# Gate and up weights in 4 MB transfers from the ninth expert on, and a shorter shift of the shared down piece

## The chip, the cores and the metric

The kernel runs on one NeuronCore of one Trainium2 chip. The metric is the device time of that core in microseconds (us). Everything is float32.

## What is computed

A transformer block on 256 tokens of width 1024: a token mixer (sparse attention beside an mLSTM), a cross-attention to 256 memory tokens, and a mixture of 32 experts with the top 4 chosen per token. The change concerns the experts alone. For every expert `e`, in the reference:

```
def expert_block(args):
    xb, e = args
    gu = xb @ w_gu[e] + b_gu[e]
    g, u = gu[:, :D_FF], gu[:, D_FF:]
    g = jnp.minimum(g, SWIGLU_LIMIT)
    u = jnp.clip(u, -SWIGLU_LIMIT, SWIGLU_LIMIT)
    return ((u + 1.0) * (g * jax.nn.sigmoid(SWIGLU_ALPHA * g))) @ w_down[e] + b_down[e]
```

`w_gu[e]` is 1024 x 2048 (8 MB) and `w_down[e]` is 1024 x 1024 (4 MB), so the 32 experts read 32 x 12 MB of weights, each byte once.

## The kernel before, in words

The mixer and the cross-attention come first. Then come 32 expert blocks, numbered here from 0, one for each expert, with 64 token slots each; the text says "block 14" for the work on expert 14. In a block TensorE multiplies the gathered tokens (`r_memT`, the stationary operand, 128 x 64) with the weights as moving operand: four gate-and-up pieces `gu0` to `gu3` (16 matmuls of 128 x 512 each, two rows `k` of the contraction per partition), then the scatter of the block before (L1377), two turns of the places (L1484), the gather of tokens for a later block (L1361, not in blocks 30 and 31), the transposes of the hidden values (L1489), the biases (L1458), then two down pieces `dn0` and `dn1`. Between the last gate-and-up piece and `dn0` VectorE and ScalarE compute the activation; TensorE's own work fills most of that time.

Each piece is one transfer of 2 MB: 128 partitions with one unbroken run of 16 KB each. SyncE (SP) issues all of them on one queue, served in order, and each transfer is spread over 16 DMA engines, 8 runs on each.

The buffers for weights are 11 slots of 2 MB. Even experts use `gu0` to `gu3` and `dn0` in `ring` (semaphores `loaded[s]`, `freed[s]`), odd experts use `r_odd[0]` to `r_odd[3]` for `gu0` to `gu3` and a part of `r_gbx` for `dn0` (`odd_loaded[j]`, `odd_freed[j]`). The eleventh slot, in `ring`, holds `dn1` of every expert: the shared down piece. The first five pieces of an expert are called its heads here. Before SP issues a piece it waits until TensorE has used what stood in that slot (two experts earlier for heads, one expert earlier for `dn1`); all that stands behind it in SP's program waits with it.

The order of the queue is written out by hand. In its first part (up to expert 11's heads) `dn1` of expert e stands behind all five heads of expert e + 1, so that TensorE gets `dn1` late. Then a shift: in each of five steps `dn1` moves one piece forward. After it `dn1` of an expert stands right behind its own heads.

```
for k in range(1, HEADS + 1):
    e = 2 * AHEAD + 1 + k
    if k > 1:
        heads(e, range(HEADS + 1 - k, HEADS))
    if k < HEADS:
        heads(e + 1, range(HEADS - k))
    others(e)
```

`others(i)` waits for the shared slot and issues `dn1` of expert i. `piece_rows` is where TensorE waits for a piece. For expert 31 `gu3`, `dn0` and `dn1` come in halves.

Of the kernel before, what the change touches and what calls it, by code (L numbers as in the profile page):

```python
# [40 lines left out]
NE, TOPK = 32, 4  # L41
SLOTS = 64
# [32 lines left out]
AHEAD = 5  # L75

# [78 lines left out]
def program(nc, A, out):  # L155
    ctx = ExitStack()
    with ctx:
# [11 lines left out]
        r_odd = [sb(f"r_odd{j}", [P, SLOT_W]) for j in range(4)]  # L169
# [150 lines left out]
        x_rows = r_x[:].rearrange("p (t j q k) -> p t j k q", t=TT, j=4, k=2)  # L320
# [99 lines left out]
        gu_dram = A["w_gu"].rearrange("l e (j p k) n -> (l e) j p k n", k=2, p=P)  # L420
# [7 lines left out]
        def _(sp):  # L428
# [67 lines left out]

            def expert_piece(e, j):
                name = EXPERT_PIECES[j]
                s = eslot[name]
                if j < 4:  # L500
                    dst, src = ring[:, s].rearrange("p (k n) -> p k n", k=2), gu_dram[e, j]
                else:
                    dst, src = ring[:, s].rearrange("p (k n) -> p k n", k=4), dn_dram[e, j - 4]
# [7 lines left out]
            def odd_half(e, j, k):  # L511
                sp.dma_start(odd_slot[j][:, k], gu_dram[e, j][:, k]).then_inc(odd_loaded[j], 16)

            def odd_piece(e, j):
                sp.dma_start(odd_slot[j], gu_dram[e, j] if j < 4 else dn_dram[e, j - 4]).then_inc(odd_loaded[j], 16)  # L515
# [153 lines left out]
        def _(act):  # L669
# [136 lines left out]
            act.dma_start(gain2.rearrange("p (j k) -> p j k", k=2), A["g_ffn"][0].rearrange("(j p k) -> p j k", p=P, k=2))\  # L806
# [1376 lines left out]
```

## Time and profile before

| | |
|---|---|
| time, median of 3 runs | 1281.8 us (1279.98 to 1282.27) |
| profiled execution, its own time | 1279.55 us |
| its span | 1277.8 us |
| mean granted TensorE clock | 0.995 of full speed |
| TensorE busy (matmuls) | 1227.0 us, 96% |
| VectorE, ScalarE, GpSimd busy | 25%, 11%, 1% |
| DMA over the span | 454.69 MB, mean 356 GB/s |

The span is measured from the first to the last instruction of one profiled execution. The busy share of matmuls includes the pipelining of one matmul into the next, so 96% doesn't mean that nothing can be gained elsewhere. The page cuts the span into 40 slices of 32 us; of these the last 28, from about 380 us on, are the expert blocks.

### The profile page before, as it was taken

Reading aid. Unit: us, or ns where it says so; the run is one execution under the profiler, and the core shown is the slowest. Engines: PE = TensorE matmul, PEld = TensorE weight load, DVE = VectorE, ACT = ScalarE, POOL = GpSimd, SP = SyncE. Lnnn points to the kernel's source line nnn. Section 1 sums busy time; section 2 is a strip of 40 time slices with the busy share of each in tenths; the row PEclk is TensorE's granted clock in tenths of the full one; section 3 lists DMA queues with packets and bytes.
Section 4 is the critical chain, followed back from the end, with each engine's and each line's share of the span. In section 5 each row is a group of like instructions: output and inputs, shape, how many; then the busy total and the mean of one; then the engine's idle time right before and its main releaser. Section 6 shows DMA issues by size and latency. Waiting matters only on the chain.

```text
span 1277.8 us, 14901 instructions
## 1 busy us (share of the span) xinstructions
PE 1227.0 (96%) x6163; PEld 603.2 (47%) x6163; DVE 324.3 (25%) x733; ACT 145.2 (11%) x325; POOL 8.1 (1%) x34
## 2 busy tenths in 40 slices
PE   9999999999999999999989999999998999999987
PEld 8868885858544333334333333433333344333322
DVE  2362334370732111212111111211111132211112
ACT  2223332002210000000000000000000000000001
POOL 1000000000000000000000000000000000000000
PEclk9999999999999999999999999999999999999999
DMA  9953233257489999999999999999999999999996
GB/s 333 310 214 132 83 116 132 99 202 278 169 341 429 425 430 428 426 428 427 430 429 428 428 427 431 429 428 427 427 430 430 428 426 427 428 428 427 427 428 270
DMA packets 60595, 454.69 MB, mean 356 GB/s; under 512 B 7244, under 2 KB 14088, under 8 KB 35080
## 3 DMA queue, kind: packets, MB, share of 16 engines
q1 hardware_dynamic: 58312, 452.49, 86.2%
q10 hardware_dynamic: 2240, 1.58, 0.4%
q8 instruction: 33, 0.54, 0.2%
q14 instruction: 10, 0.08, 0.0%
HBM read 453.00 MB, written 1.05 MB: 355 GB/s over the span
## 4 chain that ended last, share of the span: by engine, by line
PE 70%; DMA 28%; SPq 1%; DVE 1%; issue 1%; ACT 0%; DVEq 0%; ACTq 0%
PE ps L1384 32%; DMA r_odd<-in_w_gu_dram 16%; PE ps L914 13%; DMA ring<-in_w_down_dram 12%; PE ps L1234 4%; PE ps L921 3%; PE ps L1361 3%; PE ps L1377 3%; PE ps L1458 2%; PE ps L967 1%; PE ps L1489 1%; PE ps L1484 1%; PE ps L1305 1%; PE ps L1287 1%; SPq L515 1%
## 5 line engine op out<-in xcount | busy, mean ns | idle before, releaser
L1384 PE MATMUL ps<-ring,r_memT 128*64 128x512 f32 x1024 | 225.8, 594 | 13.2 <-DMA ring<-in_w_gu_dram 12.4
L1384 PE MATMUL ps<-r_odd,r_memT 128*64 128x512 f32 x1024 | 225.4, 594 | 12.5 <-DMA r_odd<-in_w_gu_dram 12.5
L1384 PE MATMUL ps<-ring,r_kx 128*64 128x512 f32 x768 | 176.9, 609 | 13.0 <-DMA ring<-in_w_down_dram 13.0
L2080 DVE TENSOR_SCALAR r_ga<-ps 128x512 f32<-128x512 f32 x32 | 22.1, 692 | 636.7 <-PE ps L1384 636.7
L1384 PEld LDWEIGHTS ps<-r_odd,r_memT 128*64 128x64 f32 x1024 | 72.9, 137 | 162.5 <-issue 135.6
L1384 PEld LDWEIGHTS ps<-ring,r_memT 128*64 128x64 f32 x1024 | 71.9, 137 | 161.3 <-issue 135.6
L914 PE MATMUL ps<-r_odd,ring 128*128 128x256 f32 x576 | 128.0, 380 | 0.0
L1384 PEld LDWEIGHTS ps<-ring,r_kx 128*64 128x64 f32 x768 | 54.9, 140 | 132.3 <-issue 108.3
L914 PEld LDWEIGHTS ps<-r_odd,ring 128*128 128x128 f32 x576 | 108.5, 190 | 16.8 <-issue 2.3
L855 ACT ACTIVATE r_ga<-r_ga 128x512 f32<-128x512 f32 x32 | 20.2, 630 | 460.0 <-DVE r_ga L2080 460.0
L1361 PE MATMUL ps<-r_dm,r_x 128*128 128x128 f32 x512 | 65.8, 282 | 0.0
L1377 PE MATMUL ps<-r_kx,r_dm 64*128 64x512 f32 x256 | 63.6, 615 | 0.7 <-ACT r_kx L861 0.7
L1361 PEld LDWEIGHTS ps<-r_dm,r_x 128*128 128x128 f32 x512 | 62.8, 197 | 1.6 <-DVE r_dm L2010 0.8
L1384 PE MATMUL ps<-r_gbx,r_kx 128*64 128x512 f32 x256 | 58.5, 598 | 0.8 <-DVE r_kx L2093 0.8
L861 ACT ACTIVATE r_kx<-ps 128x512 f32<-128x512 f32 x32 | 19.1, 597 | 335.9 <-PE ps L1384 335.9
L1377 PEld LDWEIGHTS ps<-r_kx,r_dm 64*128 64x128 f32 x256 | 22.0, 186 | 41.3 <-issue 39.7
L2018 DVE TENSOR_TENSOR r_memT<-ps,sm 128x512 f32<-128x512 f32 x32 | 22.1, 692 | 64.6 <-PE ps L1361 64.6
L1384 PEld LDWEIGHTS ps<-r_gbx,r_kx 128*64 128x64 f32 x256 | 17.0, 136 | 40.6 <-issue 27.4
L1458 PE MATMUL ps<-r_ga,r_kx 32*64 32x512 f32 x256 | 35.8, 612 | 0.0
L914 PE MATMUL ps<-r_memT,ring 128*128 128x256 f32 x128 | 28.5, 381 | 0.0
L1234 PE MATMUL ps<-ring,r_odd 128*128 128x512 f32 x64 | 27.8, 592 | 0.0
L914 PEld LDWEIGHTS ps<-r_memT,ring 128*128 128x128 f32 x128 | 24.0, 190 | 3.8 <-issue 0.7
(358 smaller groups left out, 834.1 us busy)
## 6 DMA issues: line engine op xcount, KB each, us to landing
ring<-in_w_gu_dram SPq DMA_DIRECT2D x63, 2048.0 KB, 27.0
r_odd<-in_w_gu_dram SPq DMA_DIRECT2D x60, 2048.0 KB, 28.2
ring<-in_w_down_dram SPq DMA_DIRECT2D x47, 2048.0 KB, 22.6
r_gbx<-in_w_down_dram SPq DMA_DIRECT2D x15, 2048.0 KB, 28.5
ring<-in_w_in_dram SPq DMA_DIRECT2D x7, 2048.0 KB, 14.0
r_odd<-in_w_gu_dram SPq DMA_DIRECT2D x8, 1024.0 KB, 14.5
ring<-in_w_k_x_dram SPq DMA_DIRECT2D x2, 2048.0 KB, 10.5
ring<-in_w_v_x_dram SPq DMA_DIRECT2D x2, 2048.0 KB, 8.0
```

The source lines that it names most:

```text
L515: sp.dma_start(odd_slot[j], gu_dram[e, j] if j < 4 else dn_dram[e, j - 4]).then_inc(odd_loaded[j], 16)
L855: nc.scalar.activation(sig, gact, ACT.Sigmoid, scale=1.702).then_inc(sig_done, 1)
L861: nc.scalar.activation(y_slot, ps[:, ZBK, :], ACT.Copy).then_inc(yslot_ready, 1)
L914: last = mm(o[:, j * T:(j + 1) * T], w(k), src[:, k, :], start=(k == 0), stop=(k == kk - 1))
L921: last = mm(o, src[:, k, t * P:(t + 1) * P], w[:, k, 0:n], start=(k == 0), stop=(k == C - 1))
L1234: last = mm(o, lhs(k), rhs[:, k], start=(k == 0), stop=(k == 3), skip_group_check=True)
L1361: last = mm(ps[:, buf, c * P:(c + 1) * P], x_rows[:, t, 2 * q + c // 2, c % 2], place[:, t], start=(t == 0), stop=(t == 1))
L1377: last = mm(ps[:, YB + 2 * t + n, :], scat[half, t * P:(t + 1) * P], y_slot[half, :], start=False, stop=False, skip_group_check=True)
L1384: last = mm(ps[n * SLOTS:(n + 1) * SLOTS, bk, :], stationary_, moving(n), start=start, stop=stop, skip_group_check=True)
L1458: mm(ps[n * SLOTS:(n + 1) * SLOTS, GBK + b, :], cur[q * NE:(q + 1) * NE, :], bgu_rows[q * NE:(q + 1) * NE, :], start=True, stop=False, ski ...
L2018: V.tensor_tensor(xg[:, buf, 4 * q:4 * q + 4], ps[:, bank_, :].rearrange("p (c s) -> p c s", c=4), gain_half[q], ALU.mult).then_inc(xg_rea ...
L2080: V.tensor_scalar(gact, ps[:, GBK, :], 7.0, None, ALU.min).then_inc(g_limited, 1)
```

## The change

Three things change in the transfers, and one in the layout that goes with them.

1. The contraction index of `w_gu` is laid on partitions with four rows per partition instead of two (`(q p k)` with k=4), so that two neighbouring pieces of an expert are one region of 4 MB with 32 KB per partition. For experts 0 to 7 and in part for expert 31 `gu_part` still loads a 2 MB half of it (16 KB out of each 32 KB). From expert 8 on `even_pair` and `odd_pair` load `gu0` with `gu1` and `gu2` with `gu3` in one transfer. To have neighbouring slots the four `r_odd` tensors become one, `r_odds`.
2. SP issues a pair when the second of its two slots is free. TensorE waits for the pair at its first piece, and no longer at the second (`second`).
3. The shift of `dn1` has three steps in place of five: `dn1` of expert 12 stands behind four pieces of expert 13 as before, that of expert 13 behind two pieces of expert 14 (before: three), that of expert 14 directly behind its own heads (before: behind two pieces of expert 15).
4. The gather's stationary operand `x_rows` and the gain `gain2` follow the new index: their elements are taken from `r_x` in steps of 4 (before: 2). TensorE's blocks 4 to 7 stand outside the loop.

```diff
-        gu_dram = A["w_gu"].rearrange("l e (j p k) n -> (l e) j p k n", k=2, p=P)
+        gu_dram = A["w_gu"].rearrange("l e (q p k) n -> (l e) q p k n", k=4, p=P)
...
-        x_rows = r_x[:].rearrange("p (t j q k) -> p t j k q", t=TT, j=4, k=2)
+        x_rows = r_x[:].rearrange("p (t q r k) -> p t q k r", t=TT, q=2, k=4)
...
+            def gu_part(e, j):
+                return gu_dram[e, j // 2][:, 2 * (j % 2):2 * (j % 2) + 2]
+
+            def even_pair(e, q):
+                s = eslot[EXPERT_PIECES[2 * q]]
+                assert eslot[EXPERT_PIECES[2 * q + 1]] == s + 1
+                dst = ring[:, s:s + 2].rearrange("p s (k n) -> p (s k) n", k=2)
+                sp.dma_start(dst, gu_dram[e, q]).then_inc(loaded[s], 16)
+
+            def odd_pair(e, q):
+                dst = r_odds[:, 2 * q:2 * q + 2].rearrange("p s (k n) -> p (s k) n", k=2)
+                sp.dma_start(dst, gu_dram[e, q]).then_inc(odd_loaded[2 * q], 16)
...
-            with sp.Fori(1, AHEAD + 1) as p:
+            def odd_pairs(p):
+                for q in range(2):
+                    sp.wait_ge(odd_freed[2 * q + 1], p)
+                    odd_pair(p * 2 + 1, q)
+                sp.wait_ge(odd_freed[4], p)
+                odd_piece(p * 2 + 1, 4)
...
-            for k in range(1, HEADS + 1):
+            def part_of(e, k):
+                if k == 2:
+                    s = eslot["dn0"]
+                    sp.wait_ge(odd_freed[4] if e % 2 else freed[s], e // 2)
+                    odd_piece(e, 4) if e % 2 else expert_piece(e, 4)
+                else:
+                    sp.wait_ge(odd_freed[2 * k + 1] if e % 2 else freed[eslot[EXPERT_PIECES[2 * k + 1]]], e // 2)
+                    odd_pair(e, k) if e % 2 else even_pair(e, k)
+
+            for k in range(1, 4):
                 e = 2 * AHEAD + 1 + k
-                if k > 1:
-                    heads(e, range(HEADS + 1 - k, HEADS))
-                if k < HEADS:
-                    heads(e + 1, range(HEADS - k))
+                for part in range(4 - k, 3):
+                    if k > 1:
+                        part_of(e, part)
+                for part in range(3 - k):
+                    part_of(e + 1, part)
                 others(e)
...
-            for j in range(HEADS):
-                sp.wait_ge(odd_freed[j], NE // 2 - 1)
-                if j < 3:
-                    odd_piece(NE - 1, j)
-            in_halves(odd_slot[3], gu_dram[NE - 1, 3], 2, odd_loaded[3], rest_loaded[0])
+            sp.wait_ge(odd_freed[1], NE // 2 - 1)
+            odd_pair(NE - 1, 0)
+            sp.wait_ge(odd_freed[3], NE // 2 - 1)
+            odd_piece(NE - 1, 2)
+            in_halves(odd_slot[3], gu_part(NE - 1, 3), 2, odd_loaded[3], rest_loaded[0])
+            sp.wait_ge(odd_freed[4], NE // 2 - 1)
...
-            def piece_rows(j, uses, odd):
-
+            def piece_rows(j, uses, odd, paired=True, last_expert=False):
+
+                second = paired and j in (1, 3)
                 if odd and j < HEADS:
-                    pe.wait_ge(odd_loaded[j], uses * 16 + (32 if j < 3 else 16))
+                    if j == 3 and last_expert:
+                        pe.wait_ge(odd_loaded[3], ALONE // 2 * 16 + 16)
+                    elif not second:
+                        pe.wait_ge(odd_loaded[j], uses * 16 + (32 if j < 3 else 16))
                     return lambda k, a: odd_slot[j][:, k, a:a + 512]
                 s = eslot[EXPERT_PIECES[j]]
-                pe.wait_ge(loaded[s], uses * 16 + (16 * dmas[s] + 16))
+                if not second:
+                    pe.wait_ge(loaded[s], uses * 16 + (16 * dmas[s] + 16))
...
-            four_blocks(0)
-            with pe.Fori(1, 6) as n:
+            for n in range(ALONE // 4):
+                four_blocks(n)
+            with pe.Fori(ALONE // 4, 6) as n:
                 four_blocks(n)
```

On SP, the shift in the kernel before begins with four pieces of expert 13; then come `dn1` of 12, `dn0` of 13, three pieces of expert 14, `dn1` of 13, `gu3` and `dn0` of 14, two pieces of 15 and `dn1` of 14 (`ring<-in_w_down_dram` is `dn1` of any expert and `dn0` of an even one, `r_gbx<-in_w_down_dram` is `dn0` of an odd one):

```order
L515 DMA r_odd<-in_w_gu_dram 128x4096 x4
L504 DMA ring<-in_w_down_dram 128x4096
L515 DMA r_gbx<-in_w_down_dram 128x4096
L504 DMA ring<-in_w_gu_dram 128x4096 x3
L504 DMA ring<-in_w_down_dram 128x4096
L504 DMA ring<-in_w_gu_dram 128x4096
L504 DMA ring<-in_w_down_dram 128x4096
L515 DMA r_odd<-in_w_gu_dram 128x4096 x2
L504 DMA ring<-in_w_down_dram 128x4096
```

In the changed kernel the same place on SP is the whole shift: both pairs of 13, `dn1` of 12, `dn0` of 13, the first pair of 14, `dn1` of 13, the second pair of 14, and then `dn0` and `dn1` of 14:

```order
L510 DMA r_odds<-in_w_gu_dram 128x8192 x2
L519 DMA ring<-in_w_down_dram 128x4096
L530 DMA r_gbx<-in_w_down_dram 128x4096
L506 DMA ring<-in_w_gu_dram 128x8192
L519 DMA ring<-in_w_down_dram 128x4096
L506 DMA ring<-in_w_gu_dram 128x8192
L519 DMA ring<-in_w_down_dram 128x4096 x2
```

`dn1` of 14 has moved ahead of the two pieces of 15, and `dn1` of 13 ahead of `gu2` of 14.

On TensorE (PE), in the loop over blocks of the kernel before, the gate-and-up part of an even block waits for each of its four pieces (`loaded4`, `loaded5`, `loaded0`, `loaded1` are the slots of `gu0` to `gu3`):

```order
L1384 MATMUL ps<-ring,r_memT 64x512 [waits loaded4]
L1384 MATMUL ps<-ring,r_memT 64x512 x7
L1450 REGISTER_ALU
L1384 MATMUL ps<-ring,r_memT 64x512 [waits loaded5]
L1384 MATMUL ps<-ring,r_memT 64x512 x7
L1450 REGISTER_ALU
L1384 MATMUL ps<-ring,r_memT 64x512 [waits loaded0]
L1384 MATMUL ps<-ring,r_memT 64x512 x7
L1384 MATMUL ps<-ring,r_memT 64x512 [waits loaded1]
```

In the changed kernel the same part of the loop on TensorE has two waits:

```order
L1434 MATMUL ps<-ring,r_memT 64x512 [waits loaded4]
L1434 MATMUL ps<-ring,r_memT 64x512 x15
L1505 REGISTER_ALU
L1434 MATMUL ps<-ring,r_memT 64x512 [waits loaded0]
L1434 MATMUL ps<-ring,r_memT 64x512 x15
```

The waits for `gu1` and `gu3` are gone, and `gu0` now waits until `gu1` is there as well.

## Rows read from the trace of the kernel before

**Rows 1.** The page: GB/s in 40 slices, and TensorE's down matmuls

```profile
GB/s 333 310 214 132 83 116 132 99 202 278 169 341 429 425 430 428 426 428 427 430 429 428 428 427 431 429 428 427 427 430 430 428 426 427 428 428 427 427 428 270
L1384 PE MATMUL ps<-ring,r_kx 128*64 128x512 f32 x768 | 176.9, 609 | 13.0 <-DMA ring<-in_w_down_dram 13.0
```

**Rows 2.** DMA packets of two expert blocks, 960 to 1018.74 us

```profile
DMA packets 1728, 25.17 MB, mean 428 GB/s; under 512 B 192, under 2 KB 192, under 8 KB 192
```

**Rows 3.** DMA packets from 50 to 60 us, rows of 2 KB

```profile
DMA packets 1918, 3.87 MB, mean 387 GB/s; under 512 B 30, under 2 KB 30, under 8 KB 1918
```

**Rows 4.** The chain of waits, transfer of `dn1` of block 11: start, length

```profile
675.03 25.49 DMA ring<-in_w_down_dram
```

**Rows 5.** SP in time: issues of dn1 of 12, 13, 14

```profile
705.95 0.33 SPq L504 DMA_DIRECT2D ring<-in_w_down_dram  x1
...
732.39 0.33 SPq L504 DMA_DIRECT2D ring<-in_w_down_dram  x1
...
758.81 0.33 SPq L504 DMA_DIRECT2D ring<-in_w_down_dram  x1
```

**Rows 6.** TensorE at `dn1` of blocks 7, 8, 10, 11: start, length, [idle before]

```profile
583.07 3.65 PE L1384 MATMUL ps<-ring,r_kx 128*64 128x512 f32 x16 [1.01 <-DMA ring<-in_w_down_dram]
...
612.45 5.31 PE L1384 MATMUL ps<-ring,r_kx 128*64 128x512 f32 x16 [2.72 <-DMA ring<-in_w_down_dram]
...
671.20 3.65 PE L1384 MATMUL ps<-ring,r_kx 128*64 128x512 f32 x16 [2.71 <-DMA ring<-in_w_down_dram]
...
700.56 5.35 PE L1384 MATMUL ps<-ring,r_kx 128*64 128x512 f32 x16 [2.73 <-DMA ring<-in_w_down_dram]
```

**Rows 7.** TensorE in a late block, from gu3 on

```profile
960.03 3.65 PE L1384 MATMUL ps<-r_odd,r_memT 128*64 128x512 f32 x16 [1.25 <-DMA r_odd<-in_w_gu_dram]
963.61 1.99 PE L1377 MATMUL ps<-r_kx,r_dm 64*128 64x512 f32 x8
...
969.27 3.65 PE L1384 MATMUL ps<-r_gbx,r_kx 128*64 128x512 f32 x16
...
976.19 7.08 PE L1384 MATMUL ps<-ring,r_memT 128*64 128x512 f32 x32
984.50 3.65 PE L1384 MATMUL ps<-ring,r_memT 128*64 128x512 f32 x16 [1.24 <-DMA ring<-in_w_gu_dram]
...
1018.77 3.65 PE L1384 MATMUL ps<-r_odd,r_memT 128*64 128x512 f32 x16 [1.24 <-DMA r_odd<-in_w_gu_dram]
```

**Rows 8.** SP: two issues into a queue that had run empty

```profile
377.74 0.33 SPq L504 DMA_DIRECT2D ring<-in_w_gu_dram  x1
...
381.17 0.33 SPq L504 DMA_DIRECT2D ring<-in_w_gu_dram  x1
```

**Rows 9.** The same two transfers, 377 to 383 us: time to landing

```profile
ring<-in_w_gu_dram SPq DMA_DIRECT2D x1, 2048.0 KB, 7.7
...
ring<-in_w_gu_dram SPq DMA_DIRECT2D x1, 2048.0 KB, 9.1
```

**Rows 10.** TensorE from gu3 of block 30 to the scatter of block 31

```profile
1225.86 3.65 PE L1384 MATMUL ps<-ring,r_memT 128*64 128x512 f32 x16 [1.24 <-DMA ring<-in_w_gu_dram]
1229.44 1.99 PE L1377 MATMUL ps<-r_kx,r_dm 64*128 64x512 f32 x8
...
1233.52 7.09 PE L1384 MATMUL ps<-ring,r_kx 128*64 128x512 f32 x32
1240.63 3.65 PE L1384 MATMUL ps<-r_odd,r_memT 128*64 128x512 f32 x16
...
1255.84 1.94 PE L1384 MATMUL ps<-r_odd,r_memT 128*64 128x512 f32 x8 [0.15 <-DMA r_odd<-in_w_gu_dram]
1257.71 1.99 PE L1377 MATMUL ps<-r_kx,r_dm 64*128 64x512 f32 x8
```

**Rows 11.** Weight loads in steps of 2 (L1361) and of 4 (L1489)

```profile
L1361 PEld LDWEIGHTS ps<-r_dm,r_x 128*128 128x128 f32 x512 | 62.8, 197 | 1.6 <-DVE r_dm L2010 0.8 <-issue 0.8
...
L1489 PEld LDWEIGHTS ps<-ident,r_kx 128*128 128x128 f32 x128 | 17.8, 204 | 0.7 <-DVE r_kx L2089 0.7
```

More of the change, by code:

```diff
@@ L75 @@
 AHEAD = 5
+ALONE = 8
 FILL = [("ga", n) for n in range(4)] + [("gb", n) for n in range(4)] + \
@@ L168, in program @@
         r_x = sb("r_x", [P, TT * D])
-        r_odd = [sb(f"r_odd{j}", [P, SLOT_W]) for j in range(4)]
+        r_odds = sb("r_odds", [P, 4, SLOT_W])
+        r_odd = [r_odds[:, j] for j in range(4)]
         r_gbx = sb("r_gbx", [P, 1672 + SLOT_W])
@@ L500, in expert_piece @@
                 if j < 4:
-                    dst, src = ring[:, s].rearrange("p (k n) -> p k n", k=2), gu_dram[e, j]
+                    dst, src = ring[:, s].rearrange("p (k n) -> p k n", k=2), gu_part(e, j)
                 else:
@@ L511, in odd_half @@
             def odd_half(e, j, k):
[L512 removed]
+                sp.dma_start(odd_slot[j][:, k], gu_part(e, j)[:, k]).then_inc(odd_loaded[j], 16)
             def odd_piece(e, j):
[L515 removed]
+                sp.dma_start(odd_slot[j], gu_part(e, j) if j < 4 else dn_dram[e, j - 4]).then_inc(odd_loaded[j], 16)
             def odd_heads(p, part=range(HEADS)):
@@ L560, in _, with even_pairs @@
             sp.wait_ge(first_half_freed, 1)
-            sp.dma_start(rows2[:, 0], gu_dram[2, 0][:, 0]).then_inc(first_half_loaded, 16)
+            sp.dma_start(rows2[:, 0], gu_part(2, 0)[:, 0]).then_inc(first_half_loaded, 16)
             sp.wait_ge(freed[s], 1)
-            sp.dma_start(rows2[:, 1], gu_dram[2, 0][:, 1]).then_inc(loaded[s], 16)
+            sp.dma_start(rows2[:, 1], gu_part(2, 0)[:, 1]).then_inc(loaded[s], 16)
             even_heads(1, range(1, HEADS))
             others(1)
-            with sp.Fori(1, AHEAD + 1) as p:
+            def odd_pairs(p):
[4 more added lines that the diff above has]
+                odd_piece(p * 2 + 1, 4)
+            def even_pairs(p):
+                for q in range(2):
+                    sp.wait_ge(freed[eslot[EXPERT_PIECES[2 * q + 1]]], p)
+                    even_pair(p * 2, q)
+                sp.wait_ge(freed[eslot["dn0"]], p)
+                expert_piece(p * 2, 4)
+            with sp.Fori(1, ALONE // 2 - 1) as p:
                 odd_heads(p)
@@ L605, in _ @@
                     e = sp.value_load(cnt_i[0:1, bass.ds(i - (NE - 1), 1)], min_val=0, max_val=NE - 1)
-                    for j in range(6):
+                    for q in range(2):
+                        sp.wait_ge(freed[eslot[EXPERT_PIECES[2 * q + 1]]], i - NE // 2)
+                        even_pair(e, q)
+                    for j in (4, 5):
                         sp.wait_ge(freed[eslot[EXPERT_PIECES[j]]], i - NE // 2 if j < HEADS else i)
@@ L1360, in gather_half @@
                     for t in range(TT):
-                        last = mm(ps[:, buf, c * P:(c + 1) * P], x_rows[:, t, 2 * q + c // 2, c % 2],
+                        last = mm(ps[:, buf, c * P:(c + 1) * P], x_rows[:, t, q, c],
                                   place[:, t], start=(t == 0), stop=(t == 1))
@@ L1368, in gather_late @@
                     for t in range(TT):
-                        last = mm(ps[:, XBK, c * SLOTS:(c + 1) * SLOTS], x_rows[:, t, c // 2, c % 2],
+                        last = mm(ps[:, XBK, c * SLOTS:(c + 1) * SLOTS], x_rows[:, t, c // 4, c % 4],
                                   place[:, t, 0:SLOTS], start=(t == 0), stop=(t == 1))
@@ L1467, in gate_up @@
                         pe.wait_ge(first_half_loaded, 16)
-                    w = piece_rows(j, heads_used if j < HEADS else i, odd)
+                    w = piece_rows(j, heads_used if j < HEADS else i, odd, not (isinstance(i, int) and i < ALONE),
+                                   is_block(i, NE - 1))
                     for k in range(2):
```

17 lines of the change are left out of this document (13 added, 4 removed).

## The prediction

> **What bounds the kernel now.** I read the page's GB/s line first: from slice 13 to slice 39 every slice moves 425 to 431 GB/s [rows 1]. The queue of weight transfers never pauses in the expert blocks, so their length is bytes over rate plus what stands after the last transfer. Then TensorE in time: in a late block it waits 1.24 us at `gu2` and again at `gu3`, each time for a transfer, and two blocks take 1018.77 - 960.03 = 58.74 us, 29.37 each [rows 7]. TensorE's own work in a block is `gu3` 3.58 (960.03 to 963.61), the middle part 5.66 (to 969.27), the down pieces 6.92 (to 976.19) and three more pieces at 3.46: 26.54 us. It has 2.83 us to spare per block. So only three things can move the time: the rate of the stream, a hole in it, and TensorE's work after the last landings. Last I read how the stream's time divides over packets [rows 2, 3], how SP's issues stand to landings in the shift [rows 4, 5], and the tail [rows 10].
>
> **Term 1, longer runs.** In two late blocks 1728 packets pass, 192 of them the small ones that report completion [rows 2]: 1536 runs of 16 KB, 96 per DMA engine, 58740 / 96 = 611.9 ns each. From 50 to 60 us the queue is full as well, with runs of 2 KB: (1918 - 30) / 16 = 118 runs per engine in 10 us, 84.7 ns each [rows 3]. The difference, 527.2 ns for 14336 bytes, is 27.2 bytes per ns; 2048 bytes then take 75.3 ns and 9.4 ns are left as a gap per run. By this a 2 MB piece takes 8 x 612.0 = 4.90 us and a pair in 32 KB runs 8 x (1205.2 + 9.4) = 9.72 us instead of 9.79. An expert saves 16 gaps, 0.150 us; experts 8 to 30 and one pair of 31 are 23.5 experts: 3.5 us saved. If the completion packets cost a gap too, two fewer per expert and engine add 0.4: 3.9. The lower bound is nothing, if the loss is not per run. I take 3.5, since the two stretches differ in run length above all.
>
> The Trainium skill, page "DMA: Bandwidth & Descriptors", section "Why small descriptors are slow (HBM only)", gives a fixed overhead of about 3 cycles per packet, with 850 MHz in its section "Where 436 GB/s comes from"; as an estimate from that page a gap would be 3.5 ns, the saving 23.5 x 16 x 3.5 = 1.3 us, and my sum below would be 2.2 us higher. The measured gap is nearly three times that, and I go by it.
>
> **Term 2, a hole at the second step of the shift.** SP may issue `dn1` of 14 only when TensorE has used `dn1` of 13. That does not move with the change: TensorE runs without a wait from the landing of `dn1` of 11 (675.03 + 25.49 = 700.52 [rows 4]) to this issue at 758.81 [rows 5], 58.3 us. What the queue still holds does. Before, two pieces of 15 stood ahead of `dn1` of 14; the queue then had twelve pieces after `dn1` of 11 up to `dn0` of 14, and these two: 14 x 4.90 = 68.5 us, 10.2 more than the 58.3. Now the queue ends with `dn0` of 14: four pairs and four single pieces, 4 x 9.72 + 4 x 4.90 = 58.45 us, 0.15 us after the issue. Is that too late? A transfer issued at 377.74 into an empty queue landed after 7.7 us; the next, issued at 381.17 and 4.3 us before that landing, after 9.1, that is 4.8 us behind it [rows 8, 9]. So 4.3 us ahead is early enough, and with nothing ahead 7.7 - 4.9 = 2.8 us of start and report are seen. Taking the hole as 2.8 minus the margin: 2.65 us. But the 58.3 us hold a slow `dn1` of 11: 5.35 us with the granted clock at half in it, where the same work takes 3.65 elsewhere [rows 6]. Of the three waits of 2.7 us shown there two were followed by such a stretch, the third was not; after 1.0 us there was none. Without it TensorE is 1.7 us earlier, the margin is 1.85 and the hole 0.95. Bounds: 0 (engines still at work on the last runs when the new ones come) and 2.8. I take 0.95. The other issues of the shift have room: `dn1` of 13 at 732.39 is 31.9 after the landing of 11 and the queue reaches to 38.9 (three pairs, two pieces); `dn1` of 15 comes 26.4 after that of 14 and the queue grows meanwhile by 29.2. SP's issues for later pairs stand behind it, and none is needed before.
>
> **Term 3, the tail.** Before, TensorE took `gu0` as it landed and had `gu3` alone to do after the last gate-up landing. With pairs it starts both halves when the second is there. Count from the landing of the second pair of 30 (the time at which `gu3` of 30 lands now): two pieces 7.04, then scatter, turns, transposes and biases 4.08 (1229.44 to 1233.52), down pieces 7.11 (to 1240.63) [rows 10]: 18.2 us. The first pair of 31 lands 2 x 4.90 + 9.72 = 19.5 after, so TensorE waits for it. Then four pieces follow without a wait, since `gu2` and the halves of `gu3` are there before they are wanted: 13.9 us, end at 33.45. Before, the scatter of block 31 begins at 1257.71, 31.85 after 1225.86. So 1.6 us lost. If TensorE's clock drops after its wait ahead of that block's second pair, 1.7 more makes 19.9 in place of 19.5, and the loss is 2.0.
>
> In the steady blocks the wait becomes one piece of 29.22 - 26.54 = 2.7 us ahead of the second pair, as long as the waits after which the clock fell in rows 6, and no longer two or more of 1.24. A slow stretch costs 1.7 and fits into the 2.7: the stream still sets the pace. Pairs gated by their second slot are no danger to the stream: `dn1` is used 6.92 + 5.66 + 7.04 us after the second pair landed, 9.8 after its own landing, with 24.4 us of heads queued: 14.5 us ahead.
>
> **Costed at nothing.** `x_rows` in steps of 4: TensorE's weight loads go from 197 to about 204 ns, as those of L1489, which takes such steps [rows 11]; they lie under the matmuls. The first eight blocks are issued as before. TensorE's unrolled code is fetched beside 12 MB per block. The waits dropped at `gu1` and `gu3` would have been fulfilled. If the weight loads had no cover, 7 ns x 512 would be 3.6 us of TensorE time, spread over blocks with 2.7 us to spare.
>
> **Sum.** -3.5 + 0.95 + 1.6 = -1.0 us; with the clock low at both places -3.5 + 2.65 + 2.0 = +1.1. Against the profiled execution's 1279.55 that is 1278.6 to 1280.7; the median of the runs stands 2.25 higher, so 1280.8 to 1282.9. I forecast 1281.0: no change. A measurement of this kernel tells about 0.2%, 2.6 us, from no change.
>
> **Rivals.**
> - *Full saving, nothing given back.* The hole closes, since DMA engines run several packets at once, and the tail's lag shrinks. 3.5 to 3.9 us less: 1277.9 to 1278.3, faster. For it: queue and TensorE miss each other by 0.15 us only. Against: the tail's 1.6 is TensorE's own arithmetic. 0.15.
> - *No saving per run.* A 32 KB run is moved as two packets of 16 KB, or the loss is not per run. Then +0.95 + 1.6 = 2.5, up to 4.6 with the low clock: 1284.3 to 1286.4, slower or at its edge. For it: no run of 32 KB stands in the trace. Against: the 2 KB stretch. Each ns of gap is worth 23.5 x 16 ns = 0.38 us, so with both slow stretches (4.6 without a saving) it decides from a gap below 5 ns. 0.14.
> - *The wider pitch costs rate.* Partitions now read 32 KB apart, engines at once twice as far apart as before. From the rows: each 1% of rate on the pairs is 23.5 x 19.4 x 0.01 = 4.6 us, so a rate lower by 0.8% undoes the saving and turns -1.0 into +2.6, which decides; at 2% it is +8 and the time 1290. For it: nothing in the trace; 2 KB rows at other pitches lose only what the gap explains. 0.07. The Trainium skill, same page, section "Latency and other measured facts", reports copies slowing when partitions lie at large powers of two apart, by about 3% at 512 KiB, and no run here shows that.
> - *The stream starves later.* SP waits for both slots, TensorE lags after its slow stretches and after the extra tables in block 24, and holes of some 3 us come more than once: 1285 to 1288. Against: 14.5 us of queue. 0.06.
> - The forecast: 0.58, of which 0.05 lies beyond -2.6 us and 0.04 beyond +2.6.
>
> **Range and chances.** The range reaches to most of the first two rivals and to the low edges of the others: 1277.6 to 1285.4. Faster 0.15 + 0.05 and a little for a gap above my estimate: 0.22. Slower: 0.04, most of the no-saving case (0.10), 0.07 and 0.06 minus their mild ends: 0.24. Same 0.54.
>
> **What would show it.** Right: packets of 32 KB in the late blocks and a rate near 430; two late blocks in 58.4 us; one wait of 2.7 us per block at the second pair, sometimes followed by a low clock; one slice of the DMA line short near 757 us; SP's issue of `dn1` of 14 with the queue nearly empty; `gu0` to `gu3` of block 31 in one row of some 13.9 us. Wrong: packets still at 16 KB, a rate of 428 or below, more than one hole, or a last block in which TensorE waits for halves of `gu3`.

## The result, and the profile of the changed kernel

The changed kernel takes 1294.27 us (median of 5 runs, 1293.2 to 1295.39) and the kernel before 1281.73 (5 runs, 1279.98 to 1282.27). The ratio is 1.01, its 95% interval 1.0088 to 1.0111: slower by some 12.5 us, which is clear of the noise. The prediction said no change, 1277.6 to 1285.4 us. The times of the kernel before lie in two clusters, near 1279.8 and near 1282.2 us, so that its median jumps between them from one set of runs to the next; below, small differences are therefore read from the ratios, each 0.001 of which is 1.28 us.

From the page of the changed kernel: the span, the busy time of each engine, GB/s in 40 slices of 32.3 us, and the shares of the chain of work that ended last:

```profile
span 1291.4 us, 14741 instructions
PE 1274.6 (99%) x6163; PEld 667.0 (52%) x6163; DVE 324.3 (25%) x733; ACT 145.2 (11%) x325; POOL 8.0 (1%) x34
GB/s 331 317 200 130 98 98 130 98 240 275 163 307 407 426 428 429 428 429 429 434 430 427 424 318 429 435 426 435 427 433 425 430 430 433 428 433 429 430 425 238
PE 94%; DMA 5%; DVE 1%; issue 0%; ACT 0%; SPq 0%; DVEq 0%; ACTq 0%
```

TensorE was busy for 1227.0 us before and is now busy for 1274.6, with the same 6163 matmuls. From the 14th slice on the rate is not lower than before [rows 1], but for one short slice, the 24th (742 to 775 us). The last line is the surprise: the chain runs on TensorE for 94% of the span and hardly touches a DMA (before: 70% and 28%). So the question is which matmuls take 47.6 us more. The groups by line and shape, 365 to 1290 us (busy us, mean ns of one | idle us before them):

```profile
L1434 PE MATMUL ps<-ring,r_memT 128*64 128x512 f32 x1024 | 223.8, 593 | 0.8 <-issue 0.7
L1434 PE MATMUL ps<-r_odds,r_memT 128*64 128x512 f32 x1024 | 222.8, 592 | 2.1 <-DMA r_odds<-in_w_gu_dram 2.1
L1434 PE MATMUL ps<-ring,r_kx 128*64 128x512 f32 x768 | 171.1, 594 | 0.0
L1411 PE MATMUL ps<-r_dm,r_x 128*128 128x128 f32 x512 | 124.8, 397 | 0.0
L1411 PEld LDWEIGHTS ps<-r_dm,r_x 128*128 128x128 f32 x512 | 121.9, 328 | 1.6 <-DVE r_dm L2067 0.8 <-issue 0.8
L1545 PEld LDWEIGHTS ps<-ident,r_kx 128*128 128x128 f32 x128 | 21.3, 228 | 0.5 <-DVE r_kx L2146 0.5
L1540 PEld LDWEIGHTS ps<-ident,r_dm 128*128 128x128 f32 x64 | 6.4, 140 | 24.4 <-issue 24.4
```

The same gather group and TensorE's waits of the kernel before, for comparison (total us, times, longest):

```profile
L1361 PE MATMUL ps<-r_dm,r_x 128*128 128x128 f32 x512 | 65.8, 282 | 0.0
...
PE ps L1384 <- DMA ring<-in_w_down_dram: 13.0, 6, 2.7
PE ps L1384 <- DMA r_odd<-in_w_gu_dram: 12.5, 11, 1.3
PE ps L1384 <- DMA ring<-in_w_gu_dram: 12.4, 10, 1.2
```

The gather, whose stationary operand is now taken from `r_x` in steps of 4, went from 65.8 to 124.8 us: 59.0 us more for 512 matmuls. Its weight loads went from 197 [rows 11] to 328 ns. (The records of neighbouring matmuls overlap, so 282 and 397 ns are not the pace.) Against that TensorE lost 37.9 us in waits for transfers before and 2.1 now. Busy time +47.6 and waits -35.8 give +11.8 us; the last scatter starts at 1281.46 in place of 1269.42, 12.0 later. (Busy time rose by less than 59 mainly because the matmuls on the experts' weights, lines L1384 and L1434, take 676.2 us in sum in place of 686.6: with the waits went the slow-clock stretches behind some of them and the fresh starts behind the others. The granted clock rose from 0.995 to 0.999.)

In time, TensorE in two late blocks of the changed kernel, and the gather of before:

```profile
954.31 3.89 PE L1411 MATMUL ps<-r_dm,r_x 128*128 128x128 f32 x16
...
966.57 13.91 PE L1434 MATMUL ps<-r_odds,r_memT 128*64 128x512 f32 x64
980.41 1.99 PE L1427 MATMUL ps<-r_kx,r_dm 64*128 64x512 f32 x8
982.33 0.44 PE L1540 MATMUL ps<-ident,r_dm 128*128 128x128 f32 x2
982.60 3.89 PE L1411 MATMUL ps<-r_dm,r_x 128*128 128x128 f32 x16
986.33 0.63 PE L1545 MATMUL ps<-ident,r_kx 128*128 128x128 f32 x4
986.89 1.09 PE L1513 MATMUL ps<-r_ga,r_kx 32*64 32x512 f32 x8
...
994.87 13.98 PE L1434 MATMUL ps<-ring,r_memT 128*64 128x512 f32 x64
```

```profile
965.80 2.05 PE L1361 MATMUL ps<-r_dm,r_x 128*128 128x128 f32 x16
967.69 0.63 PE L1489 MATMUL ps<-ident,r_kx 128*128 128x128 f32 x4
```

From gather to gather 982.60 - 954.31 = 28.29 us pass, without a wait. The gather itself lasts 3.73 us to the next operation (982.60 to 986.33), where it was 1.89 (965.80 to 967.69): from the start of one matmul to the next 233 ns in place of 118. Here the answer to a puzzle stands too: 1.84 us more per block is less than the 2.83 us that TensorE had to spare in late blocks [rows 7]. But it did not have them everywhere. In the kernel before the first blocks run at TensorE's own pace of 26.4 us (the scatters of blocks 0 to 4 start at 409.34, 435.75, 462.15, 488.56 and 515.01), living on the pieces loaded ahead, and so do blocks 13 to 17 (the scatters of blocks 12 and 17 start at 746.02 and 878.15, 26.4 per block). Over all 32 blocks the slack was the waits and the slower matmuls behind them, about 37.9 + 10.4 = 48 us, and the edit asked for 59.

### The profile page after: what moved, and what is told of

Read it like the earlier page. It is cut to its first block, busy times and chain, and to the rows that moved or that the text cites. A ratio compares the mean times of both kernels' runs of the same rounds, so it can differ in the third digit from the quotient of the medians.

```text
span 1291.4 us, 14741 instructions
## 1 busy us (share of the span) xinstructions
PE 1274.6 (99%) x6163; PEld 667.0 (52%) x6163; DVE 324.3 (25%) x733; ACT 145.2 (11%) x325; POOL 8.0 (1%) x34
## 4 chain that ended last, share of the span: by engine, by line
PE 94%; DMA 5%; DVE 1%; issue 0%; ACT 0%; SPq 0%; DVEq 0%; ACTq 0%
PE ps L1434 48%; PE ps L964 13%; PE ps L1411 9%; DMA r_odds<-in_w_gu_dram 5%; PE ps L1427 4%; PE ps L1284 4%; PE ps L971 3%; PE ps L1513 2%; PE ps L1545 1%; PE ps L1017 1%; PE ps L1540 1%; PE ps L1355 1%; PE ps L1337 1%; PE ps L1184 0%; PE ps L1249 0%; DMA r_x<-in_x_dram 0%
## 5 line engine op out<-in xcount | busy, mean ns | idle before, releaser
L1434 PE MATMUL ps<-r_odds,r_memT 128*64 128x512 f32 x1024 | 222.8, 592 | 2.1 <-DMA r_odds<-in_w_gu_dram 2.1
L1434 PE MATMUL ps<-ring,r_memT 128*64 128x512 f32 x1024 | 223.8, 593 | 0.8 <-issue 0.7
L1434 PE MATMUL ps<-ring,r_kx 128*64 128x512 f32 x768 | 171.1, 594 | 0.0
L1434 PEld LDWEIGHTS ps<-r_odds,r_memT 128*64 128x64 f32 x1024 | 75.5, 137 | 146.8 <-issue 145.2
L1434 PEld LDWEIGHTS ps<-ring,r_memT 128*64 128x64 f32 x1024 | 74.1, 137 | 144.6 <-issue 142.0
L964 PE MATMUL ps<-r_odds,ring 128*128 128x256 f32 x576 | 128.0, 380 | 0.0
L1411 PE MATMUL ps<-r_dm,r_x 128*128 128x128 f32 x512 | 124.8, 397 | 0.0
L1411 PEld LDWEIGHTS ps<-r_dm,r_x 128*128 128x128 f32 x512 | 121.9, 328 | 1.6 <-DVE r_dm L2067 0.8
L964 PEld LDWEIGHTS ps<-r_odds,ring 128*128 128x128 f32 x576 | 108.5, 190 | 16.8 <-issue 2.3
L1434 PEld LDWEIGHTS ps<-ring,r_kx 128*64 128x64 f32 x768 | 54.7, 137 | 112.9 <-issue 106.4
L1434 PE MATMUL ps<-r_gbx,r_kx 128*64 128x512 f32 x256 | 58.5, 598 | 0.8 <-DVE r_kx L2150 0.8
L1434 PEld LDWEIGHTS ps<-r_gbx,r_kx 128*64 128x64 f32 x256 | 17.2, 136 | 40.6 <-issue 34.0
L1513 PE MATMUL ps<-r_ga,r_kx 32*64 32x512 f32 x256 | 35.8, 612 | 0.0
L964 PE MATMUL ps<-r_memT,ring 128*128 128x256 f32 x128 | 28.5, 381 | 0.0
L1284 PE MATMUL ps<-ring,r_odds 128*128 128x512 f32 x64 | 27.8, 592 | 0.0
## 6 DMA issues: line engine op xcount, KB each, us to landing
r_odds<-in_w_gu_dram SPq DMA_DIRECT2D x8, 1024.0 KB, 14.2
```

Source lines behind the costliest of these rows:

```text
L964: last = mm(o[:, j * T:(j + 1) * T], w(k), src[:, k, :], start=(k == 0), stop=(k == kk - 1))
L1284: last = mm(o, lhs(k), rhs[:, k], start=(k == 0), stop=(k == 3), skip_group_check=True)
L1411: last = mm(ps[:, buf, c * P:(c + 1) * P], x_rows[:, t, q, c], place[:, t], start=(t == 0), stop=(t == 1))
L1434: last = mm(ps[n * SLOTS:(n + 1) * SLOTS, bk, :], stationary_, moving(n), start=start, stop=stop, skip_group_check=True)
L1513: mm(ps[n * SLOTS:(n + 1) * SLOTS, GBK + b, :], cur[q * NE:(q + 1) * NE, :], bgu_rows[q * NE:(q + 1) * NE, :], start=True, stop=False, ski ...
```

## Experiments

**1. Which part costs: the transfers or the gather.** Two kernels. Both take other columns of `r_x` than the weights' rows want, so they compute something else than the reference, and their times alone are read. The first is the changed kernel with only the gather's operand back in steps of 2 (the index in the two gather calls changes with it, not shown):

```diff
-        x_rows = r_x[:].rearrange("p (t q r k) -> p t q k r", t=TT, q=2, k=4)
+        x_rows = r_x[:].rearrange("p (t j q k) -> p t j k q", t=TT, j=4, k=2)
```

> The changed kernel with the gather's stationary operand taken from r_x in steps of 2 again, as in the kernel before; the gathered columns then don't fit the weights' new rows, so this kernel's expert values differ from the reference, and its time alone is read. Theory 1 (the gather's steps of 4 cost the time): the 16 gather matmuls of a block take 1.9 us again instead of 3.7, TensorE waits for transfers again, and the time falls from 1293 to 1280 to 1283 (the kernel before minus 3.5 for the longer runs, plus 0.95 to 2.65 for a hole at the shift, plus 1.6 to 2.0 for the tail). Theory 2 (4 MB transfers released by their second slot, the hole at the shift and the tail cost the time): it stays above 1290, since all of that is still there.

The second is the kernel before with the reverse edit, the gather in steps of 4 and nothing else in it changed:

> The kernel before with only the gather's stationary operand in steps of 4, as in the changed kernel (again the gathered columns don't fit the weights' rows; the time alone is read). Theory 1: TensorE's block is 26.4 + 1.85 = 28.3 us; TensorE has work from 368 us to the end nearly without a wait, so the time is that of the changed kernel less its wait at block 23 and 31 (2 us): 1290 to 1293. Theory 2: 28.3 us fit under the 29.4 us in which a block's weights arrive, so the time is within 3 us of the kernel before, 1281 to 1285.

Measured, with 1281.88 us for the kernel before on the same chip (27 runs): the pairs with steps of 2 take 1282.29 (1281.44 to 1283.81, 11 runs), ratio 1.0012 (1.0003 to 1.0021); the kernel before with steps of 4 takes 1290.03 (1289.56 to 1290.69, 4 runs), ratio 1.0075 (1.0059 to 1.009). By the ratios the gather alone makes the kernel before slower by 9.6 us (7.6 to 11.5), and without it the transfers cost 1.5 (0.4 to 2.7). Together that is 11.1, against 12.8 (11.3 to 14.2) for the whole change. In the kernel before with steps of 4 the group is the same as in the changed one, and so is the loss of waits, one being left:

```profile
L1361 PE MATMUL ps<-r_dm,r_x 128*128 128x128 f32 x512 | 124.8, 397 | 0.0
L1361 PEld LDWEIGHTS ps<-r_dm,r_x 128*128 128x128 f32 x512 | 121.9, 328 | 1.6 <-issue 0.8 <-DVE r_dm L2010 0.8
...
1260.70 7.09 PE L1384 MATMUL ps<-r_odd,r_memT 128*64 128x512 f32 x32 [1.59 <-DMA r_odd<-in_w_gu_dram]
```

**2. Is it the step, and from which on.** The kernel before with the gather in steps of 1, 3 and 8, one run each; these too compute something else than the reference. Each changes one line of the layout and the index in two calls (not shown), for instance for steps of 8:

```diff
-        x_rows = r_x[:].rearrange("p (t j q k) -> p t j k q", t=TT, j=4, k=2)
+        x_rows = r_x[:].rearrange("p (t r c) -> p t c r", t=TT, c=C)
```

> The kernel before with the gather's stationary operand contiguous in r_x (other columns than the weights' rows want; read for its durations). If what costs is that each element of a weight load stands on a line of 16 bytes of its own, steps of 1 and of 2 are alike: 16 gather matmuls in 1.9 us, weight loads of 190 ns and 197 ns. If the cost grows with the step itself, steps of 1 are faster than steps of 2, well under 1.9 us.

> The kernel before with steps of 3 elements (12 bytes) in the gather's stationary operand; durations only. Lines of 16 bytes: three of four elements open a new line, so weight loads lie between 197 and 329 ns, nearer to the latter, near 260 to 300. Cost growing with the step: halfway, 263.

> The kernel before with steps of 8 elements (32 bytes) in the gather's stationary operand; durations only. Lines of 16 bytes: no more than steps of 4 cost, loads of 329 ns, 16 gather matmuls in 3.7 us, time as with steps of 4, 1288 to 1291. Cost growing with the step: loads of 500 ns and more, a gather of 6 us and more, time above 1340.

The groups of the gather, in the kernels with steps of 1, 3 and 8 in this order:

```profile
L1361 PE MATMUL ps<-r_dm,r_x 128*128 128x128 f32 x512 | 62.6, 275 | 0.0
L1361 PEld LDWEIGHTS ps<-r_dm,r_x 128*128 128x128 f32 x512 | 59.7, 192 | 1.6 <-DVE r_dm L2010 0.8 <-issue 0.8
```

```profile
L1361 PE MATMUL ps<-r_dm,r_x 128*128 128x128 f32 x512 | 94.3, 338 | 0.0
L1361 PEld LDWEIGHTS ps<-r_dm,r_x 128*128 128x128 f32 x512 | 91.3, 261 | 1.6 <-DVE r_dm L2010 0.8 <-issue 0.8
```

```profile
L1361 PE MATMUL ps<-r_dm,r_x 128*128 128x128 f32 x512 | 127.6, 402 | 0.0
L1361 PEld LDWEIGHTS ps<-r_dm,r_x 128*128 128x128 f32 x512 | 124.7, 334 | 1.6 <-DVE r_dm L2010 0.8 <-issue 0.8
```

| step (fp32 elements) | weight load, ns | 512 gather matmuls, busy us | time of the kernel, us |
|---|---|---|---|
| 1 | 192 | 62.6 | 1279.43 (one run) |
| 2 (before) | 197 | 65.8 | 1281.73 |
| 3 | 261 | 94.3 | 1281.34 (one run) |
| 4 | 328 | 124.8 | 1290.03 |
| 8 | 334 | 127.6 | 1294.39 (one run) |

The load's time rises between steps 2 and 4 and then all but stays. A cost that grows with the step itself is excluded by step 8 (334 ns; 500 and more were expected of it). What fits is a cost per 16 bytes touched: per element, 0.25 such units are touched at step 1, 0.5 at step 2, 0.75 at step 3 and 1 from step 4 on, if from step 2 down something else sets the 192 to 197 ns. Step 3 lies in the middle between its neighbours, at 261 ns between 197 and 328, as both readings expected, so it does not tell them apart. The unit of 16 bytes is inferred from these five times; no run tested it in another way, such as another type or another start of the operand. The Trainium skill, page "SBUF — State Buffer", section "Door 1: The DMA port swizzle", says that SBUF has 16-byte cachelines, that at least two hits per line are needed for full bandwidth, and that each crossing into a new line pays; it names fp32's limit as 4. The trace agrees with the two hits: 197 ns at two elements per line, 328 at one. It does not agree with a limit of 4: a step of 4 is not free here, it is where the full price is reached.

Step 3 has 28.5 us more TensorE work and, in one run, the time of before. That is the slack of 48 us at work: in that run TensorE still waits 19.4 us for transfers, about what 48 - 28.5 leaves. Step 4 asks for 59 and shows.

Step 8 cost 4 us more than step 4 in its single run, above the 1288 to 1291 expected, with 2.8 us more in the gather; the rest was not followed up.

**3. The hole and the tail, with the gather out of the way.** Starting from the kernel with pairs and steps of 2, first the shift in four steps instead of three (`part_of(e, k)` issues the first pair, the second pair or `dn0` of expert e; what follows the shift is renumbered, not shown):

```diff
-            for k in range(1, 4):
-                e = 2 * AHEAD + 1 + k
-                for part in range(4 - k, 3):
-                    if k > 1:
-                        part_of(e, part)
-                for part in range(3 - k):
+            for e, own, ahead in ((12, (), (0, 1)), (13, (2,), (0,)), (14, (1, 2), (0,)), (15, (1, 2), ())):
+                for part in own:
+                    part_of(e, part)
+                for part in ahead:
                     part_of(e + 1, part)
                 others(e)
```

> As the changed kernel with the gather in steps of 2, and with four steps in the shift: dn1 of 14 stands behind the first pair of 15, dn1 of 15 behind its own heads. If the hole at the second step of the shift is worth what the prediction says, 0.95 to 2.65 us less than the same kernel with three steps, and every slice of the DMA line from 13 on at 425 GB/s or more. If the DMA engines bridge a late issue by themselves, no difference.

Then, on top of it, `gu2` and `gu3` of expert 30 and `gu0` and `gu1` of expert 31 as single pieces (SP's part; TensorE's waits for these pieces change with it, not shown):

```diff
+            even_pair(NE - 2, 0)
+            for j in (2, 3, 4):
+                sp.wait_ge(freed[eslot[EXPERT_PIECES[j]]], NE // 2 - 1)
+                expert_piece(NE - 2, j)
+            others(NE - 2)
...
-            sp.wait_ge(odd_freed[1], NE // 2 - 1)
-            odd_pair(NE - 1, 0)
+            for j in range(2):
+                sp.wait_ge(odd_freed[j], NE // 2 - 1)
+                odd_piece(NE - 1, j)
```

> As the one before, and gu2 and gu3 of expert 30 and gu0 and gu1 of expert 31 in transfers of 2 MB, each waited for by itself. If the tail costs what the prediction says: 1.6 to 2.0 us less than the kernel without this edit (some 0.1 us of it is lost again to shorter runs), and then 1277.5 to 1279.5 in all, 3 us less than the kernel before, which is what the longer runs save. If the saving per run isn't there: not below 1280.5.

Measured: 1280.61 us (1279.46 to 1283.53, 11 runs) for the first, ratio 0.9998 (0.9989 to 1.0008), and 1279.04 (1278.1 to 1281.41, 11 runs) for both, ratio 0.9989 (0.998 to 0.9998). By the ratios the hole was worth 1.8 us and the tail 1.1 (by the medians 1.7 and 1.6; by the means of the 11 runs each 1.5 and 1.4, uncertain by some 1 us each), and what is left of the pairs is a gain of 1.4 us (0.3 to 2.6), where 3 had been expected. The part of the stream itself can be read from the bytes that it moved from 840 to 1225 us, in the kernel before and in the last one:

```profile
DMA packets 11314, 164.74 MB, mean 428 GB/s; under 512 B 1259, under 2 KB 1259, under 8 KB 1259
```

```profile
DMA packets 7761, 165.51 MB, mean 430 GB/s; under 512 B 863, under 2 KB 863, under 8 KB 863
```

0.77 MB more in 385 us is 1.8 us' worth at 430 GB/s, for 13.2 experts of 12.58 MB: 0.14 us per expert, where the prediction has 0.150. GB/s in 40 slices, with three steps of the shift and then with four:

```profile
GB/s 333 314 208 132 86 113 132 99 213 273 165 351 429 427 426 428 427 430 429 433 431 430 430 384 438 427 429 437 428 426 430 430 430 436 429 429 426 432 424 233
```

```profile
GB/s 334 322 200 132 73 125 132 99 203 274 169 341 425 428 427 427 428 430 430 431 431 430 431 428 423 434 431 428 431 427 431 431 433 432 426 430 436 426 424 225
```

The slice that is short at 384 is the 24th; with four steps it reads 428. The stretch of 750 to 760 us alone (us, busy us of PE, PEld, DVE, ACT and POOL, granted clock, DMA share, GB/s), again three steps and then four:

```profile
750.00:760.00 10.00, 10.00 (x52) 3.29 (x46) 2.10 (x8) 0.60 (x1) 0.00 (x0) 1.00 0.76 290
```

```profile
750.00:760.00 10.00, 10.00 (x53) 3.42 (x54) 2.60 (x8) 0.60 (x1) 0.00 (x0) 1.00 1.00 429
```

290 against 429 for 10 us is 3.2 us' worth of bytes in the queue, more than the 1.8 us by which the times differ; each ratio is uncertain by some 1.2 us, and part of the loss may be made good later. TensorE in late blocks and in the tail of the kernel with three steps of the shift:

```profile
1185.85 7.09 PE L1434 MATMUL ps<-r_odds,r_memT 128*64 128x512 f32 x32
1195.46 8.78 PE L1434 MATMUL ps<-r_odds,r_memT 128*64 128x512 f32 x32 [2.53 <-DMA r_odds<-in_w_gu_dram]
...
1224.69 7.09 PE L1434 MATMUL ps<-ring,r_memT 128*64 128x512 f32 x32 [0.90 <-DMA ring<-in_w_gu_dram]
...
1244.29 13.95 PE L1434 MATMUL ps<-r_odds,r_memT 128*64 128x512 f32 x64 [1.41 <-DMA r_odds<-in_w_gu_dram]
1258.17 1.99 PE L1427 MATMUL ps<-r_kx,r_dm 64*128 64x512 f32 x8
```

This is the steady block that the prediction described: one wait of 2.5 us at the second pair, a stretch of 8.78 in place of 7.09 us behind it with the granted clock low, and `gu0` to `gu3` of block 31 in one row of 13.95.

**4. The longer runs with the valid layout, and the shift and tail of experiment 3.** The changed kernel with both edits of experiment 3, gather in steps of 4, which computes the reference:

> The changed kernel with its gather in steps of 4, and with the two edits that saved 3.3 us in the steps-of-2 version: four steps in the shift and single pieces at the end of the queue. Theory 1 (TensorE sets the end from the gather's steps): closing the hole saves nothing by itself; only the two waits of TensorE that the trace after shows, 0.7 and 1.4 us, can go, so 1291.5 to 1293, still 10 us over the kernel before. Theory 2 (the stream's holes set the end): 6.5 us of hole and more come back, 1286 to 1288.

It took 1290.01 us (1289.24 to 1291.23, 4 runs), ratio 1.0072 (1.0055 to 1.0089), with 1280.53 (7 runs) for the kernel before: the same as the 1290.03 of the kernel before with steps of 4, and between the two times expected. In its expert blocks TensorE waits for no transfer, so what the stream gains is worth nothing. The four steps do not close the hole in this kernel, as they did in experiment 3; they move it. 10 us of the changed kernel and 10 us of this one, with the same columns as above:

```profile
760.00:770.00 10.00, 10.00 (x53) 3.66 (x54) 2.69 (x8) 0.60 (x1) 0.00 (x0) 1.00 0.31 113
```

```profile
790.00:800.00 10.00, 10.00 (x50) 3.42 (x47) 0.00 (x0) 0.60 (x1) 0.00 (x0) 1.00 0.37 129
```

SP waits for TensorE's use of `dn1` before it issues the next, and TensorE's blocks take 28.3 us here. The kernel before with steps of 4 has short slices at this place too (407 and 380 GB/s), with the old order of the queue.

The changed kernel takes 4.3 us more than this one by the medians, 3.6 by the ratios. The scatters in time show where most of it comes in. The scatter of block 0 starts at 414.30 here and at 414.82 in the changed kernel, 0.5 later, and that difference stays the same, block by block, up to the one that starts at 980.41 there. In block 23 TensorE has caught up with the stream in the changed kernel and waits for a pair: up to 1030 us its queues moved 348.67 MB, and those of this experiment's kernel 349.31, 1.5 us' worth more. In block 31, where this experiment's kernel has single pieces, the changed one waits for a pair again:

```profile
1030.97 7.09 PE L1434 MATMUL ps<-r_odds,r_memT 128*64 128x512 f32 x32 [0.70 <-DMA r_odds<-in_w_gu_dram]
1037.99 1.99 PE L1427 MATMUL ps<-r_kx,r_dm 64*128 64x512 f32 x8
...
1255.88 13.95 PE L1434 MATMUL ps<-r_odds,r_memT 128*64 128x512 f32 x64 [1.41 <-DMA r_odds<-in_w_gu_dram]
1269.77 1.99 PE L1427 MATMUL ps<-r_kx,r_dm 64*128 64x512 f32 x8
```

The same scatters start at 1036.47 and 1266.38 in the kernel of this experiment, so the distance grows from 0.5 to 1.5 and then to 3.4 us. The two profiled runs are 3.6 us apart (1293.2 and 1289.61).

**5. The end.** From the start of the last scatter to the end of the span the kernel before takes 1277.8 - 1269.42 = 8.4 us, the changed one 1291.4 - 1281.46 = 9.9. SP's four issues of the output in the kernel before and in the changed one, and then, of the changed kernel from 1285 us on, the DMA queues (packets, MB, share of 16 engines) and the output's issues (KB each, median us to landing; 2.0 us in the kernel before):

```profile
1273.17 2.51 SPq L614 DMA_DIRECT2D out_dram<-r_x  x4
```

```profile
1285.22 3.39 SPq L664 DMA_DIRECT2D out_dram<-r_x  x4
```

```profile
q1 hardware_dynamic: 576, 1.05, 44.4%
q8 instruction: 1, 0.02, 0.9%
out_dram<-r_x SPq DMA_DIRECT2D x4, 256.0 KB, 3.1
```

A packet of instructions arrives between the output's transfers, and the four issues take 0.9 us longer. The kernels with pairs have an end of 9.8 to 10.6 us from the last scatter on, those with the old SP program one of 8.4. Two kernels tried it. The first is the last one of experiment 3 (pairs, steps of 2, shift in four steps, single pieces in the tail), with the output issued by ScalarE:

```diff
-                    sp.wait_ge(out_ready, 2 * t + n + 1)
-                    sp.dma_start(out[0, t * P:(t + 1) * P, part], x_tok[:, t, part]).then_inc(out_sem, 16)
...
+                    act.wait_ge(out_ready, 2 * t + n + 1)
+                    act.dma_start(out[0, t * P:(t + 1) * P, part], x_tok[:, t, part]).then_inc(out_sem, 16)
```

> The steps-of-2 version without hole and tail (1279.0), with the four output transfers issued by ScalarE in place of SP (the gathered columns still don't fit the weights' rows). If a fetch of SP's longer code between the output issues is what makes the end 1.5 us longer than in the kernel before, the last issue takes 0.3 to 0.4 us again and the time falls by 0.8 to 1.6 us, to 1277.5 to 1278.2, unless ScalarE's own code is fetched there. If the output transfers are slower for another reason, no difference.

The second is the kernel before with a longer SP program that does the same, two turns of a loop written out:

```diff
-            with sp.Fori(1, AHEAD + 1) as p:
+            for p in (1, 2):
+                odd_heads(p)
+                others(p * 2)
+                even_heads(p + 1)
+                others(p * 2 + 1)
+            with sp.Fori(3, AHEAD + 1) as p:
```

> The kernel before with two of SP's loop iterations written out, which issues the same transfers in the same order with some 24 more instructions in SP's program than an unrolling of none. If the fetch of SP's code is placed by the program's length alone, the end from the last scatter on may grow from 8.4 us to 9.3 to 10.6 us, as in the changed kernel, with an instruction packet between the output issues, and the time by 0.9 to 2 us, if the border falls there; if it falls elsewhere, nothing moves (1281 to 1282.5) and the trace shows no packet in the end.

Neither settled it. With ScalarE 1278.83 us (1277.65 to 1281.14, 11 runs), ratio 0.9983 (0.9974 to 0.9992) where its base has 0.9989, which the intervals don't tell apart; two instruction packets pass in its end, one of them between the four issues, which take 3.39 us. So a fetch fell there again; that it is ScalarE's program now is likely but not shown. The longer SP program gave 1281.18 (1279.6 to 1282.93, 11 runs) against 1281.48, ratio 1.0004 (0.9995 to 1.0013), its packet came before the issues, and they took 2.50 us as in the kernel before. So length alone, by this much, is not the cause. That a fetch between the issues goes with a longer end is shown by the rows; that it causes it, and what decides where the fetch falls, stays open.

## Why the prediction was wrong

**The step that failed is under "Costed at nothing": `x_rows` in steps of 4.** It said that the loads would go "from 197 to about 204 ns, as those of L1489, which takes such steps", and would "lie under the matmuls". Measured: 328 ns, not covered; 16 gather matmuls take 3.73 us in place of 1.89. This term, put at 0, was worth 9.6 us (7.6 to 11.5) of the kernel's time, and no rival named it. The row was read against the wrong neighbour. L1489 is a transpose, and a transpose's load of this size in unit steps takes 140 ns (L1484, now L1540, in the rows above), not 192. Its 204 were already 64 ns dear, and cost next to nothing there: four transposes in steps of 4 take 0.56 us (986.33 to 986.89), 140 ns each, and two in unit steps 0.27 (982.33 to 982.60), 135 each. The ordinary load takes 192 at step 1 and is not covered so: the matmul's record is 275 ns long at step 1, 282 at step 2 and 397 at step 4. Why a transpose covers its load and an ordinary matmul does not was not followed up.

**The fallback was wrong too:** "7 ns x 512 would be 3.6 us of TensorE time, spread over blocks with 2.7 us to spare". It was 59 us in place of 3.6, and 2.7 us is the slack of a late block only. The sum over the program was 48 us; a step of 3 (28.5 us more) disappears in it, and a step of 4 (59 us) doesn't.

**"It has 2.83 us to spare per block"** and "only three things can move the time" hold for the late blocks of the kernel before, not for its first blocks and blocks 13 to 17, which take 26.4 us each, and not for the changed kernel, where TensorE sets the pace nearly all the way. "The queue of weight transfers never pauses" was true; it did not mean that nothing else set the time.

**Term 1, longer runs, -3.5 us: right within the measurement.** With hole and tail mended the pairs give 1.4 us (0.3 to 2.6), and that kernel's end is 1.5 us longer (9.9 against 8.4), so the stream gave about 2.9. The bytes from 840 to 1225 us (experiment 3) give 0.14 us per expert, 3.2 for 23.5 experts. The DMA rows of a late stretch say the same in kind, 430 GB/s in place of 428 [rows 2]. Of the changed kernel from 900 to 958 us:

```profile
DMA packets 1145, 24.94 MB, mean 430 GB/s; under 512 B 128, under 2 KB 128, under 8 KB 128
```

1145 - 128 = 1017 data packets for 24.94 MB are 23.9 KB each (24523 bytes), as with one run of 32 KB for each of 16 KB. With the bytes moved, this excludes the rivals "no saving per run" and "the wider pitch costs rate".

**Term 2, the hole, 0.95 (to 2.65): 1.8 us with the gather in steps of 2,** between the two values. In the changed kernel SP's issues show it:

```profile
741.28 27.77 SPq L519 DMA_DIRECT2D ring<-in_w_down_dram  x2
769.40 0.88 SPq L510 DMA_DIRECT2D r_odds<-in_w_gu_dram  x2
```

`dn1` of 14 is the second issue of the first row, at 768.7, and the queue had been empty since 764. The prediction said that this issue time "does not move with the change"; it moved by 10 us with TensorE (in the kernel with steps of 2 it stays, at 758), and the queue then stood empty for some 6 us. TensorE, late itself, doesn't wait at that place. It waits in blocks 23 and 31, and experiment 4 does not show how much of that is the hole's, since the kernel there has a hole as well.

**Term 3, the tail, 1.6: 1.1 us** by the ratios, 1.6 by the medians; the row of 13.95 us for block 31 is as foreseen. **Missed:** 1.5 us at the end (experiment 5), whose cause stays open.

The forecast's sum for everything but the gather was -3.5 + 0.95 + 1.6 = -1.0 us; the kernel with steps of 2 measured +1.5 (0.4 to 2.7), and with the missed end the sum is +0.5. Without the gather's edit the forecast of no measurable change would have held.

## What to carry to other kernels

A change of layout changes the step of every operand that follows it: look up each such operand's load and compare it with a load of the same kind (an ordinary one with an ordinary one, a transpose with a transpose), at the same width and in the step that it will have. Here an fp32 stationary operand of 128 x 128 in steps of 4 made its matmuls take 1.9 times as long as in steps of 2 (124.8 and 65.8 us busy). And slack is to be summed over the whole program from the waits (here 48 us), not read from one late block and multiplied by the blocks. A slower TensorE also issues the transfers later, through the buffers that it frees: look for holes in the stream anew.

## What was not expected of the hardware

A weight load of 128 x 128 fp32 takes 192, 197, 261, 328 and 334 ns at steps of 1, 2, 3, 4 and 8 elements, and the matmul behind it (128 columns moving) doesn't hide it: 275, 282, 338, 397, 402. A transpose's load of that size takes 140 ns in unit steps and 204 in steps of 4 in the kernel before, at nearly the same pace (135 and 140 ns from one to the next). In the changed kernel the mean of the latter is 228, since the first of each four stands right behind the gather's slow loads (shortest, median and longest of one block):

```profile
L1545 PEld LDWEIGHTS ps<-ident,r_kx x4: 196/210/300, 986.1 to 986.6; 128*128 128x128 f32 x4
```

So a load's record depends on what stands before it, too. Runs of 32 KB moved 430 GB/s and those of 16 KB 428.

No version here that computes the reference beats the kernel before: the pairs gain some 1.4 us (2.2 with the output from ScalarE) only with the gather in steps of 2, and with the layout of the pairs it has to step by 4. A copy of `r_x` with its columns permuted might give both; it was not tried.
